# One encoder step on one core: x turned as it lands, its norm folded into the head norms and value copies, gates and late loads behind the first projection units

## The chip, the cores and the metric

The kernel runs on one core of a Trainium2 chip. TensorE does the matrix products and the turns (transposes through a product with the identity), VectorE (DVE), ScalarE (ACT) and GpSimd (POOL) do the rest, and SyncE (SP) issues nearly all DMA transfers. The metric is the device time of one execution in microseconds (us). In the profile PEld is TensorE's weight load, and SPq the issuing of transfers on SyncE.

## The reference

All is float32. 16 meta tokens, 256 prompt rows and 8 x 16 sample rows, 1024 wide, go through one layer:

```
hn = x * rsqrt(mean(x*x) + 1e-6) * attn_norm
fq, fk, fv, ff, dq, dk, dv = split(hn @ w_in)       # 512 512 512 8 512 512 512
fq, fk: rms norm of each of 8 heads of 64, gain;  logf = log_sigmoid(ff + b_forget)
dq, dk: rms norm of each head of 64, gain, rotary;  v as it is
fox:   softmax(q k / 8 + c_q - c_k, causal) v,  c = cumsum(logf)
diff:  (softmax(q1 k1 / 8) - lam softmax(q2 k2 / 8)) v, rms norm;  lam from exp of two dot products
h = x + concat(fox, diff) @ w_out
y = h + top-4-of-32 expert layer (1024 -> 2048 -> 1024) of rms(h)
```

The sample rows also see 256 cached keys and values per batch. Keys, values and logf of all rows are outputs.

## The kernel before

SBUF is one tensor, `arena`, cut by hand. The work stands in program order on each engine, joined by semaphores. There are four row tiles (`TILES`): meta (t = 0, 16 rows), two prompt tiles (t = 1, 2) and the sample tile (t = 3), 128 rows each.

**Opening.** SyncE loads x, the constants (`consts_all`, 0.6 MB, the identity in it), three gain vectors, the eight gate columns of `w_in`, block 0 of `w_in`, small gains, lambda vectors and the rotation, then blocks 1 to 5 (2 MB each, L403), the cached forget gates (L419, 32-byte runs) and the first cache rows (L425). ACT squares and sums each x tile (L687) and takes roots (L690). DVE takes reciprocals and scales x in place (L932). TensorE turns x in blocks of 128 x 128 into PSUM (L1332). ACT and DVE evacuate four blocks each per tile into `hnT`, times the gain column `gcol` (L698, L938). Then TensorE forms the gate products `w_ff` x `hnT` (L1339, 8 rows by 400 columns, 8 chunks), and DVE and ACT make the log sigmoid and its running sum from them.

**Projection.** A list `units` gives the order: blocks 0 to 4 (fox k, fox v, diff k, fox q, diff q), each for t = 1, 2, 3, so units 0 to 2 are fox k, 3 to 5 fox v, 6 to 8 diff k; then the meta tile for four blocks at once (L1375), and block 5 (diff v). A wide unit is 8 chunks of 128 x 128 weights by 512 columns (L1391). A float32 product is two instructions in the profile. For q and k units ACT squares z (L741), DVE sums by head, adds the epsilon (`ss8`, L995), ACT takes the root (L743), DVE inverts, scales z (L998) and multiplies by the gain (L1011); POOL rotates in the diff group (L575 to L579). The result stands in one of two staging buffers `zo`, from which SyncE stores it (L446) and TensorE turns it (`turn_z`, L1351, one unit late). Before writing a `zo`, `free_zo` waits for the turn and the landing of the store that used it last:

```python
if is_n(units[i]):
    eng.wait_ge(z_T, upto(is_n, i + 1))
...
if stores_on(u, o % 2):
    eng.wait_ge(s_store[o % 2], 16 * stores_on(u, o % 2))
```

ACT evacuates the turned k (L718), and for v units it copies z out (L752). `banks[4]` and `banks[5]` take the wide units in turn, so a unit waits until the unit two before it has been read.

**Later stages.** Attention (32 steps, prompt and sample), output projection, routing, and 16 pairs of experts, whose weights (24 MB a pair) run through a ring of eight 2 MB pieces. SyncE's loop refills a piece when TensorE has done with it. None of this is touched.

## Time and profile before

| | us |
|---|---|
| three runs, median (lowest to highest) | 1300.49 (1298.23 to 1304.32) |
| the profiled execution | 1307.11 |
| its span | 1305.2 |
| TensorE busy | 1234.1 (95%) |
| TensorE weight load busy | 548.7 (42%) |
| DVE / ACT / POOL busy | 356.5 / 199.0 / 157.4 |
| HBM read / written | 441.66 MB / 4.86 MB |

Durations come from the profiled execution, one run that was longer than the three timed ones. A matmul's own duration contains its way through the pipeline; a row of several instructions gives the stretch that they took together. "Idle before" is the engine's wait and what ended it.

### The profile page before, as it was taken

Reading aid. Unit: us, or ns where it says so; the run is one execution under the profiler, and the core shown is the slowest. Engines: PE = TensorE matmul, PEld = TensorE weight load, DVE = VectorE, ACT = ScalarE, POOL = GpSimd, SP = SyncE. Lnnn points to the kernel's source line nnn. Section 1 sums busy time; section 2 is a strip of 40 time slices with the busy share of each in tenths; the row PEclk is TensorE's granted clock in tenths of the full one; section 3 lists DMA queues with packets and bytes.
Section 4 is the critical chain, followed back from the end, with each engine's and each line's share of the span. In section 5 each row is a group of like instructions: output and inputs, shape, how many; then the busy total and the mean of one; then the engine's idle time right before and its main releaser. Section 6 shows DMA issues by size and latency. Waiting matters only on the chain.

```text
span 1305.2 us, 16112 instructions
## 1 busy us (share of the span) xinstructions
PE 1234.1 (95%) x6065; PEld 548.7 (42%) x6066; DVE 356.5 (27%) x944; ACT 199.0 (15%) x522; POOL 157.4 (12%) x377
## 2 busy tenths in 40 slices
PE   6799988999899999999999999999999999999997
PEld 3344445654554344343434434343434434343432
DVE  3213446451413122121412212121412212121402
ACT  5111155341401011010101001010100001010100
POOL 0011311110032020210202020120202020120000
PEclk9999997799889999999999999999999999999998
DMA  7900250585349999999999999999999999999993
GB/s 281 344 31 17 94 197 34 192 287 200 119 184 431 427 427 428 428 428 429 428 429 428 428 429 428 427 429 429 426 430 428 427 430 428 428 430 427 426 429 156
DMA packets 54537, 447.06 MB, mean 343 GB/s; under 512 B 10817, under 2 KB 11090, under 8 KB 29922
## 3 DMA queue, kind: packets, MB, share of 16 engines
q1 hardware_dynamic: 54498, 446.54, 82.4%
q8 instruction: 24, 0.39, 0.1%
q14 instruction: 15, 0.12, 0.0%
HBM read 441.66 MB, written 4.86 MB: 342 GB/s over the span
## 4 chain that ended last, share of the span: by engine, by line
PE 64%; DMA 26%; SPq 4%; DVE 2%; issue 1%; ACT 1%; POOL 1%; DVEq 0%; ACTq 0%; POOLq 0%
DMA arena<-in_w_gate_up 24%; PE psum L1685 17%; PE psum L1653 17%; PE psum L1634 7%; PE psum L1391 6%; PE psum L1556 3%; PE psum L1700 2%; SPq L403 2%; PE psum L1668 1%; PE psum L1427 1%; PE psum L1664 1%; DMA arena<-in_cache_diff_k 1%; SPq L419 1%; PE psum L1457 1%; DMA out_fox_k_p<-arena 1%
## 5 line engine op out<-in xcount | busy, mean ns | idle before, releaser
L1653 PE MATMUL psum<-arena 128*64 128x512 f32 x2048 | 450.5, 599 | 20.9 <-DMA arena<-in_w_gate_up 20.3
L1653 PEld LDWEIGHTS psum<-arena 128*64 128x64 f32 x2048 | 153.0, 138 | 316.5 <-issue 316.5
L1685 PE MATMUL psum<-arena 128*64 128x512 f32 x1024 | 224.5, 596 | 0.8
L1288 DVE TENSOR_SCALAR arena<-psum 128x256 f32<-128x256 f32 x64 | 26.7, 418 | 434.1 <-PE psum L1653 432.3
L1685 PEld LDWEIGHTS psum<-arena 128*64 128x64 f32 x1024 | 78.7, 137 | 135.7 <-issue 134.4
L1391 PE MATMUL psum<-arena 128*128 128x512 f32 x288 | 127.6, 599 | 0.0
L890 ACT ACTIVATE arena<-arena 128x256 f32<-128x256 f32 x64 | 26.7, 417 | 632.7 <-DVE arena L1288 632.7
L1634 PEld LDWEIGHTS psum<-arena 128*128 128x128 f32 x768 | 89.8, 197 | 16.1 <-issue 16.1
L1634 PE MATMUL psum<-arena 128*128 128x128 f32 x768 | 92.8, 282 | 3.8 <-POOL arena L642 3.8
L635 POOL COPY arena<-arena 128x6 f32 (+1 forms) x16 | 3.0, 188 | 761.2 <-PE psum L1685 704.6
L1700 PE MATMUL psum<-arena 128*128 128x512 f32 x192 | 93.2, 623 | 0.0
L1391 PEld LDWEIGHTS psum<-arena 128*128 128x128 f32 x288 | 54.3, 193 | 65.3 <-issue 64.6
L1306 DVE TENSOR_TENSOR arena<-psum,arena 128x512 f32<-128x512 f32 x96 | 66.5, 692 | 25.3 <-PE psum L1700 25.3
L1301 DVE COPY arena<-psum 128x512 f32<-128x512 f32 x16 | 11.1, 692 | 219.5 <-PE psum L1685 219.5
L1700 PEld LDWEIGHTS psum<-arena 128*128 128x128 f32 x192 | 28.6, 188 | 64.4 <-DVE arena L1306 42.1
L652 POOL TENSOR_SCALAR arena<-arena 128x64 f32<-128x64 f32 x96 | 53.8, 579 | 0.0
L1556 PE MATMUL psum<-arena 128*128 128x512 f32 x96 | 42.4, 595 | 1.0 <-DVE arena L1155 1.0
L642 POOL TENSOR_SCALAR arena<-arena 128x64 f32<-128x64 f32 x96 | 40.2, 443 | 0.0
L1276 DVE TENSOR_TENSOR arena<-arena 128x256 f32<-128x256 f32 x64 | 36.4, 609 | 5.4
L898 ACT ACTIVATE arena<-psum 128x512 f32<-128x512 f32 x16 | 9.6, 598 | 161.9 <-PE psum L1685 161.9
L994 DVE TENSOR_REDUCE arena<-arena 128x8 f32<-128x512 f32 (+1 forms) x14 | 9.6, 684 | 79.1 <-ACT arena L741 79.1
L1290 DVE SCALAR_TENSOR_TENSOR arena<-arena 128x256 f32<-128x256 f32 x64 | 27.3, 426 | 2.2
(225 smaller groups left out, 827.5 us busy)
## 6 DMA issues: line engine op xcount, KB each, us to landing
arena<-in_w_gate_up SPq DMA_DIRECT2D x128, 2048.0 KB, 25.2
arena<-in_w_down SPq DMA_DIRECT2D x64, 2048.0 KB, 23.0
arena<-in_w_in SPq DMA_DIRECT2D x6, 2048.0 KB, 19.8
arena<-in_cache_fox_k SPq DMA_DIRECT2D x8, 512.0 KB, 7.0
arena<-in_cache_diff_k SPq DMA_DIRECT2D x8, 512.0 KB, 6.8
arena<-in_cache_fox_v SPq DMA_DIRECT2D x8, 512.0 KB, 7.3
arena<-in_cache_diff_v SPq DMA_DIRECT2D x8, 512.0 KB, 9.4
arena<-in_w_out SPq DMA_DIRECT2D x4, 1024.0 KB, 6.2
```

Of the source, the lines that this page charges most:

```text
L642: last = nc.gpsimd.tensor_scalar(sel[u][:, t, cols], C["iota"], pRK[u][:, t, x:x + 1], None, ALU.is_equal)
L652: last = nc.gpsimd.tensor_scalar(selg[u][:, t, cols], C["iota"], pRK[u][:, t, x:x + 1], pG[u][:, t, x:x + 1], ALU.is_equal, ALU.mult)
L890: nc.scalar.activation(sg[n % 2], tg[n % 2], ACT.Sigmoid, scale=1.702).then_inc(sig_ready, 1)
L1276: nc.vector.tensor_tensor(act_rows[:, 32 * n:32 * (n + 1)], ta[n % 2].rearrange("s (p q) -> s p q", q=8), sg[n % 2].rearrange("s (p q) -> ...
L1290: lk(nc.vector.scalar_tensor_tensor(out=ta[n % 2], in0=tl[n % 2], scalar=1.0, in1=tg[n % 2], op0=ALU.add, op1=ALU.mult))
L1306: nc.vector.tensor_tensor(y[:, t, cols], banks[4 + n % 2], y[:, t, cols], ALU.add).then_inc(y_added, 1)
L1391: last = mm(z_bank(u), hnT[:, k, r0:r0 + n], wv[:, k], start=(k == 0), stop=(k == 7))
L1556: last = mm(banks[4 + n % 2], oT[:, k, P * t:P * (t + 1)], wv[:, k % 2, 512 * hf:512 * hf + 512], start=(k == 0), stop=(k == 7))
L1634: last = mm(banks[6 + k // 4][:, P * (k % 4):P * (k % 4 + 1)], x2n[:, t, P * k:P * (k + 1)], sel[u][:, t], start=(t == 0), stop=(t == 2))
L1653: last = mm(banks[n][half], XT[u][:, k, half], piece_slot(s[x])[:, c0:c0 + 512], start=False, stop=(k == 7), skip_group_check=True)
L1685: last = mm(banks[hf][half], actT[:, 4 * i + c, half], w, start=False, stop=(i == 1 and c == 3), skip_group_check=True)
L1700: mm(banks[4 + n % 2], gT[:, P * t:P * (t + 1)], rows[:, 512 * hf:512 * hf + 512], start=True, stop=True).then_inc(scat_done, 1)
```

## The change

- SyncE loads the identity alone first, then x tiles 1 and 2, block 0 in two halves with x tile 3 between, the meta rows eight times (into all 128 partitions), block 1, the other constants, gate columns, forget bias, lambda vectors, rotation, and block 2. Blocks 3, 4, 5 are issued behind the stores of units 0, 1, 2; the cached forget gates at unit 7; cache batch 0 at unit 8, batch 1 at unit 10. The three gain vectors and the four head gains are issued by ACT.
- x is turned unscaled as it lands, in the order 1, 2, 3, 0, tile 3 behind unit 0 and tile 0 behind unit 1. The row norm is not applied to x. The head norm of q and k cancels a row's scale, so only its epsilon is multiplied by (mean(x*x) + eps), as `xeps`; v is multiplied by the inverse root in its copy.
- The gate products come behind unit 2, as four column groups of 32 rows whose halves of the sum are joined and turned by four products with `pick` behind unit 3 (`gate_rows`). The gates then stand with the rows on partitions. ACT's Exp and Ln are behind unit 4, and the running sum is made on TensorE behind unit 6 (`gate_cumulate`) where DVE's scan made it before.

```diff
+X_ORDER = (1, 2, 3, 0)
+LOG_UNIT = 4
...
+    c["pick"] = np.tile(np.eye(E)[:, 0:8], (4, 1))
...
-            sp.dma_start(xs[0][0:META], io["meta_tokens"][:, :]).then_inc(s_x[0], 16)
+            sp.dma_start(ident, io["consts"][:, 0:P]).then_inc(s_ident, 16)
             for t in range(2):
                 sp.dma_start(xs[1 + t], io["x_prompt"][0, P * t:P * (t + 1), :]).then_inc(s_x[1 + t], 16)
-            sp.dma_start(xs[3], io["x_sample"].rearrange("b i n -> (b i) n")).then_inc(s_x[3], 16)
-            sp.dma_start(consts_all, io["consts"][:, :]).then_inc(s_const, 16)
-            for i, (name, n) in enumerate((("attn_norm", 8), ("ffn_norm", 8), ("diff_out_norm", 1))):
-                sp.dma_start(vecs[8 * i:8 * i + n], io[name][0].rearrange("(k p) -> k p", p=P)).then_inc(s_vec, 16)
-            sp.dma_start(gcol_x, io["ffn_norm"][0].rearrange("(p k) -> p k", p=P)).then_inc(s_gx, 16)
-
             def load_w_in(bi):
                 c0 = BLOCKS[bi][0]
                 sp.dma_start(slot(2 * bi, 2).rearrange("p (k n) -> p k n", k=8),
                              io["w_in"][0, :, c0:c0 + W].rearrange("(k p) n -> p k n", p=P)).then_inc(s_win[bi], 16)
 
+            def load_first(k0, arrived):
+                c0 = BLOCKS[0][0]
+                sp.dma_start(slot(k0 // 4).rearrange("p (k n) -> p k n", k=4),
+                             io["w_in"][0, P * k0:P * (k0 + 4), c0:c0 + W].rearrange("(k p) n -> p k n", p=P)
+                             ).then_inc(arrived, 16)
+
+            load_first(0, s_win[0])
+            sp.dma_start(xs[3], io["x_sample"].rearrange("b i n -> (b i) n")).then_inc(s_x[3], 16)
+            load_first(4, s_win0b)
+            for j in range(8):
+                sp.dma_start(xs[0][META * j:META * (j + 1)], io["meta_tokens"][:, :]).then_inc(s_x[0], 16)
+            load_w_in(1)
+            sp.dma_start(consts_all[:, P:], io["consts"][:, P:]).then_inc(s_const, 16)
             with nc.allow_non_contiguous_dma(reason="eight columns of w_in"):
-                sp.dma_start(nb_ff[0:8, 0:1], io["b_forget"][0].rearrange("(h o) -> h o", o=1)).then_inc(s_wff, 16)
-                sp.dma_start(w_ff, io["w_in"][0, :, 1536:1544].rearrange("(k p) n -> p k n", p=P)).then_inc(s_wff, 16)
-            load_w_in(0)
-            for i, name in enumerate(("fox_q_norm", "fox_k_norm", "diff_q_norm", "diff_k_norm")):
-                sp.dma_start(gains[:, i], io[name][0].partition_broadcast(P)).then_inc(s_small, 16)
+                sp.wait_ge(wff_zero, 1)
+                sp.dma_start(w_ff[:, :, 0:8], io["w_in"][0, :, 1536:1544].rearrange("(k p) n -> p k n", p=P)
+                             ).then_inc(s_wff, 16)
+            sp.dma_start(b_ff, io["b_forget"][0].partition_broadcast(P)).then_inc(s_bff, 16)
             for i, name in enumerate(("lambda_q1", "lambda_k1", "lambda_q2", "lambda_k2")):
                 sp.dma_start(lamv[:, i], io[name][0].partition_broadcast(P)).then_inc(s_small, 16)
             sp.dma_start(rot.rearrange("p t c h -> p (t c h)"), io["rot"][:, :]).then_inc(s_rot, 16)
+            load_w_in(2)
...
+            sp.dma_start(gcol_x, io["ffn_norm"][0].rearrange("(p k) -> p k", p=P)).then_inc(s_gx, 16)
...
-            for bi in range(1, 6):
-                load_w_in(bi)
-            for t in range(2):
-                sp.dma_start(lf_cache[:, t], io["cache_fox_logf"][0, :, P * t:P * (t + 1)].rearrange("b p h -> p b h")
-                             ).then_inc(s_lfc, 16)
...
-            load_cache(0, "k")
-            load_cache(0, "v")
...
+                if u < 3:
+                    load_w_in(3 + u)
+                if u == 7:
+                    for t_ in range(2):
+                        sp.dma_start(lf_cache[:, t_], io["cache_fox_logf"][0, :, P * t_:P * (t_ + 1)].rearrange("b p h -> p b h")
+                                     ).then_inc(s_lfc, 16)
+                if u == 8:
+                    load_cache(0, "k")
+                    load_cache(0, "v")
+                if u == 10:
                     sp.wait_ge(xT_done, 4)
+                    sp.wait_ge(sq_done, 2)
                     load_cache(1, "k")
                     load_cache(1, "v")
                 if u == 6:
-                    sp.wait_ge(lf_ready, 2)
+                    sp.wait_ge(lf_ready, 1)
...
+            nc.gpsimd.memset(w_ff.rearrange("p k n -> p (k n)"), 0.0).then_inc(wff_zero, 1)
...
+            for i, (name, n) in enumerate((("attn_norm", 8), ("ffn_norm", 8), ("diff_out_norm", 1))):
+                ac.dma_start(vecs[8 * i:8 * i + n], io[name][0].rearrange("(k p) -> k p", p=P)).then_inc(s_vec, 16)
+            for i, name in enumerate(("fox_q_norm", "fox_k_norm", "diff_q_norm", "diff_k_norm")):
+                ac.dma_start(gains[:, i], io[name][0].partition_broadcast(P)).then_inc(s_gains, 16)
...
-            for t in range(4):
-                n = TILES[t][1]
-                ac.wait_ge(s_x[t], 16)
-                link(nc.scalar.activation(junk[0:n], xs[t][0:n], ACT.Square, accum_out=stat[0:n, t:t + 1]))
-            nc.scalar.activation(stat[:, 8:9], stat[:, 8:9], ACT.Square).then_inc(sq_done, 1)
-            ac.wait_ge(ms_done, 1)
-            nc.scalar.activation(stat[:, 4:8], stat[:, 0:4], ACT.Sqrt).then_inc(rt_done, 1)
...
+            def x_squares(t):
+                ac.wait_ge(s_x[t], 16 if t else 128)
+                return nc.scalar.activation(junk if t else xs[0], xs[t], ACT.Square, accum_out=stat[:, t:t + 1])
+
+            for t in (1, 2):
+                hn_evac(t)
+            for t in (1, 2, 3):
+                link(x_squares(t))
+            nc.scalar.activation(stat[:, 8:9], stat[:, 8:9], ACT.Square).then_inc(sq_done, 1)
+            ac.wait_ge(ms_done, 1)
+            nc.scalar.activation(stat[:, 5:8], stat[:, 1:4], ACT.Sqrt).then_inc(rt_done, 1)
+            hn_evac(3)
+
+            def meta_rows():
+
+                hn_evac(0)
+                link(x_squares(0))
+                nc.scalar.activation(stat[:, 45:46], stat[:, 45:46], ACT.Square).then_inc(sq_done, 1)
+                ac.wait_ge(ms_done, 2)
+                nc.scalar.activation(stat[:, 4:5], stat[:, 0:1], ACT.Sqrt).then_inc(rt_done, 1)
+
+            def log_gates():
+
+                for f, i in ((ACT.Exp, 1), (ACT.Ln, 2)):
+                    ac.wait_ge(lg_v, i)
+                    nc.scalar.activation(ffl, ffl, f).then_inc(lg_a, 1)
+                    if i == 1:
+                        ac.wait_ge(lam_v, 1)
+                        nc.scalar.activation(stat[:, 10:12], stat[:, 10:12], ACT.Exp).then_inc(lam_a, 1)
...
-                    nc.scalar.activation(dst, z, ACT.Copy).then_inc(z_copied, 1)
+                    nc.scalar.activation(dst, z, ACT.Copy, scale=stat[rw, t:t + 1]).then_inc(z_copied, 1)
...
+                if u == 1:
+                    meta_rows()
+                if u == LOG_UNIT:
+                    log_gates()
...
-            for t in range(4):
-                n = TILES[t][1]
-                nc.vector.tensor_scalar(xs[t][0:n], xs[t][0:n], stat[0:n, t:t + 1], None, ALU.mult).then_inc(xn_done, 1)
...
+            def x_scales(n_, c):
+
+                cols = slice(c[0], c[-1] + 1)
+                ve.wait_ge(sq_done, n_)
+                nc.vector.tensor_scalar(stat[:, cols], stat[:, cols], 1.0 / D, EPS, ALU.mult, ALU.add).then_inc(ms_done, 1)
+                ve.wait_ge(ms_done, n_)
+                link(nc.vector.tensor_scalar(xeps[:, cols], stat[:, cols], EPS, None, ALU.mult))
+                ve.wait_ge(rt_done, n_)
+                link(nc.vector.reciprocal(stat[:, cols], stat[:, 4 + c[0]:5 + c[-1]]))
+                nc.vector.tensor_copy(stat[:, 9:10], stat[:, 8:9]).then_inc(x_scale, 1)
+
+            for t in (1, 2):
+                hn_evac(t)
+            x_scales(1, (1, 2, 3))
+            hn_evac(3)
...
+            def gate_logits():
+
+                ve.wait_ge(ff_done, 1)
+                link(nc.vector.memset(ffv, 0.0))
+                nc.vector.tensor_copy(ffc, banks[6][:, 0:NTOK]).then_inc(ff_copied, 1)
+                ve.wait_ge(ffn_done, 1)
+                ve.wait_ge(s_bff, 16)
+                for t_ in range(4):
+                    n_ = TILES[t_][1]
+                    ins = nc.vector.scalar_tensor_tensor(out=ffv[0:n_, t_], in0=banks[6][0:n_, 448 + 8 * t_:456 + 8 * t_],
+                                                         scalar=stat[0:n_, t_:t_ + 1], in1=b_ff[0:n_],
+                                                         op0=ALU.mult, op1=ALU.add)
+                link(ins)
+                link(nc.vector.tensor_scalar(ffl, ffv, -1.0, None, ALU.mult))
+                nc.vector.tensor_tensor(ffl, ffl, ffv, ALU.min).then_inc(lg_v, 1)
+
+            def gate_logs():
+
+                ve.wait_ge(lg_a, 1)
+                nc.vector.tensor_scalar(ffl, ffl, 1.0, None, ALU.add).then_inc(lg_v, 1)
+                ve.wait_ge(lg_a, 2)
+                link(nc.vector.tensor_scalar(ffv, ffv, 0.0, None, ALU.min))
+                nc.vector.tensor_tensor(lf, ffv, ffl, ALU.subtract).then_inc(lf_ready, 1)
+                ve.wait_ge(lf_ready, 1)
+                nc.vector.tensor_copy(lf_new[0:META], lf[0:META, 0:1].to_broadcast([META, 8, 8])).then_inc(lf_ready, 1)
+
+            def gate_sums():
+
+                ve.wait_ge(ncp_done, 1)
+                link(nc.vector.tensor_copy(nc_p[0:8], banks[6][0:8, 0:NKEY_P]))
+                nc.vector.tensor_copy(nc_p[32:40], nc_p[0:8]).then_inc(lf_ready, 1)
...
-                nc.vector.tensor_scalar(ss8[rw, 0], ss8[rw, 0], 1.0 / HD, EPS, ALU.mult, ALU.add).then_inc(z_ms, 1)
+                nc.vector.tensor_scalar(ss8[rw, 0], ss8[rw, 0], 1.0 / HD, xeps[rw, t:t + 1], ALU.mult, ALU.add
+                                        ).then_inc(z_ms, 1)
...
+                    hn_evac(0)
+                    x_scales(2, (0,))
+                if m == 2:
+                    lambdas()
+                    gate_logits()
+                    gate_logs()
+                    lambda_maps()
+                if m == 3:
+                    gate_sums()
...
-            pe.wait_ge(gcol_done, 1)
-            for t in range(4):
+
+            def turn_x(t):
                 n = TILES[t][1]
-                pe.wait_ge(xn_done, t + 1)
+                pe.wait_ge(s_x[t], 16 if t else 128)
                 for k in range(8):
                     last = nc.tensor.transpose(banks[2 * t + k // 4][:, P * (k % 4):P * (k % 4) + n],
                                                xs[t][0:n, P * k:P * (k + 1)], ident[0:n, 0:n])
                 last.then_inc(xT_done, 1)
-            pe.wait_ge(hnT_a, 4)
-            pe.wait_ge(hnT_v, 4)
-            pe.wait_ge(s_wff, 32)
-            for k in range(8):
-                last = mm(banks[6][0:8, 0:NTOK], w_ff[:, k], hnT[:, k], start=(k == 0), stop=(k == 7))
-            last.then_inc(ff_done, 1)
+
+            for t in (1, 2):
+                turn_x(t)
+
+            def gate_products():
+
+                pe.wait_ge(hnT_a, 4)
+                pe.wait_ge(hnT_v, 4)
+                pe.wait_ge(s_wff, 16)
+                for k in range(8):
+                    j = k % 4
+                    last = mm(banks[6][32 * j:32 * j + 32, 0:NTOK], w_ff[:, k], hnT[:, k], start=(k < 4), stop=(k >= 4))
+                last.then_inc(ff_done, 1)
+
+            def gate_rows():
+
+                pe.wait_ge(ff_copied, 1)
+                pe.wait_ge(s_const, 16)
+                for t_ in range(4):
+                    r0, n = TILES[t_]
+                    last = mm(banks[6][0:n, 448 + 8 * t_:456 + 8 * t_], ffc[:, r0:r0 + n], C["pick"], start=True, stop=True)
+                last.then_inc(ffn_done, 1)
+
+            def gate_cumulate():
+
+                pe.wait_ge(lf_ready, 1)
+                R, later = banks[6][0:8], C["cumul"][:, P:P + 1]
+                mm(R[:, 0:META], lf[0:META, 0], C["cumul"][0:META, 0:META], start=True, stop=False, skip_group_check=True)
+                mm(R[:, META:NKEY_P], lf[0:META, 0], later[0:META].to_broadcast([META, SEQ]), start=True, stop=False,
+                   skip_group_check=True)
+                mm(R[:, META:META + P], lf[:, 1], C["cumul"][:, 0:P], start=False, stop=False, skip_group_check=True)
+                mm(R[:, META + P:NKEY_P], lf[:, 1], later.to_broadcast([P, P]), start=False, stop=False,
+                   skip_group_check=True)
+                mm(R[:, META + P:NKEY_P], lf[:, 2], C["cumul"][:, 0:P], start=False, stop=True,
+                   skip_group_check=True).then_inc(ncp_done, 1)
...
+                    if u < 3:
+                        pe.wait_ge(hnT_a, u + 1)
+                        pe.wait_ge(hnT_v, u + 1)
+                    if u in (0, 1):
+                        pe.wait_ge(hnT_a, 2)
+                        pe.wait_ge(hnT_v, 2)
...
+                        if u == 0 and k == 4:
+                            pe.wait_ge(s_win0b, 16)
...
+                if u in (0, 1):
+                    turn_x((3, 0)[u])
+                if u == 2:
+                    gate_products()
+                if u == 3:
+                    gate_rows()
+                if u == 6:
+                    gate_cumulate()
```

## Rows read from the trace of the kernel before

**Rows 1.** Windows: busy us (x instructions) of each engine, granted clock, DMA share, GB/s.
```profile
6.00:8.00 2.00, 0.00 (x0) 0.00 (x0) 0.00 (x0) 1.81 (x5) 0.00 (x0) 1.00 0.99 385
...
54.00:63.30 9.30, 1.07 (x6) 1.04 (x6) 0.85 (x2) 1.09 (x2) 0.00 (x0) 0.78 1.03 355
...
64.00:66.00 2.00, 2.00 (x4) 0.94 (x3) 0.00 (x0) 0.00 (x0) 0.00 (x0) 0.50 0.86 329
66.00:68.00 2.00, 2.00 (x5) 0.83 (x5) 0.00 (x0) 0.00 (x0) 0.00 (x0) 0.97 0.07 27
...
178.40:212.00 33.60, 26.80 (x219) 16.57 (x219) 21.84 (x107) 22.52 (x83) 2.47 (x9) 1.00 0.19 63
212.00:242.00 30.00, 28.94 (x120) 18.71 (x123) 14.29 (x51) 11.12 (x46) 6.39 (x22) 0.51 0.21 72
...
370.00:1305.20 935.20, 905.34 (x4348) 371.26 (x4344) 214.25 (x455) 76.91 (x178) 97.41 (x243) 0.99 0.98 415
```
**Rows 2.** The chain that ended last: start us, us, what.
```profile
41.08 6.35 SPq L419
...
52.14 9.26 DMA out_fox_k_p<-arena
...
63.38 22.04 PE psum L1391 x48
...
132.09 6.87 PE psum L1391 x16
...
822.60 28.93 DMA arena<-in_w_gate_up
```
**Rows 3.** Timeline of all engines: start us, us, engine, line, operation, [idle before <-releaser].
```profile
2.92 1.28 ACT L687 ACT_TABLE_LOAD   x1 [2.79 <-DMA arena<-in_meta_tokens]
...
7.88 1.06 ACT L687 ACTIVATE arena<-arena 128x1024 f32<-128x1024 f32 x1 [0.15 <-DMA arena<-in_x_sample]
...
11.03 2.73 DVE L932 TENSOR_SCALAR arena<-arena 16x1024 f32<-16x1024 f32 x4
...
61.52 0.69 DVE L1011 TENSOR_TENSOR arena<-arena 128x512 f32<-128x512 f32 x1 [12.02 <-DMA out_fox_k_p<-arena]
...
62.27 1.11 PE L1351 MATMUL psum<-arena 128*128 128x128 f32 x4 [8.23 <-DVE arena L1011]
```
**Rows 4.** Timeline of TensorE's matmuls alone.
```profile
9.95 0.26 PE L1326 MATMUL psum<-arena 17*128 17x17 f32 x1 [9.95 <-DMA arena<-in_diff_out_norm]
11.92 6.32 PE L1332 MATMUL psum<-arena 16*128 16x16 f32 x32 [1.71 <-DVE arena L932]
19.50 5.55 PE L1339 MATMUL psum<-arena 128*8 128x400 f32 x16 [1.27 <-ACT arena L698]
24.98 14.00 PE L1391 MATMUL psum<-arena 128*128 128x512 f32 x32
38.91 0.36 PE L1399 MATMUL psum<-arena 8*16 8x8 f32 x4
...
148.25 7.06 PE L1375 MATMUL psum<-arena 128*16 128x512 f32 x64
```
**Rows 5.** Groups by form (busy us, mean ns), and one line's instructions (min/median/max ns).
```profile
L1332 PE MATMUL psum<-arena 128*128 128x128 f32 x24 | 5.4, 423 | 0.0
...
L698 ACT ACTIVATE arena<-psum,arena 128x128 f32<-128x128 f32 x12 | 3.4, 369 | 2.2 <-PE psum L1332 2.2
...
L1351 PE MATMUL psum<-arena x56: 207/273/475, 39.2 to 178.2; 128*128 128x128 f32 x48, 16*128 16x16 f32 x8
```
**Rows 6.** SyncE's queue (start us, us to issue), and the landing of in_x_prompt.
```profile
1.22 0.88 SPq L394 DMA_DIRECT2D arena<-in_x_prompt  x2
...
3.98 0.25 SPq L398 DMA_DIRECT2D arena<-in_diff_out_norm  x1
...
6.55 2.64 SPq L411 DMA_DIRECT2D arena<-in_fox_q_norm  x1
...
DMA to landing us min/median/max: 3.3/3.7/4.2
```

More of the change, by code:

```diff
@@ L40 @@
 Y_BASE = 6
-CONSTS = [("ident", 128), ("eye4", 32), ("smask", 16), ("ones", 128), ("iota", 64), ("own", 128), ("maps", 2),
+X_ORDER = (1, 2, 3, 0)
+LOG_UNIT = 4
+CONSTS = [("ident", 128), ("eye4", 32), ("pick", 8), ("smask", 16), ("ones", 128), ("iota", 64), ("own", 128), ("maps", 2),
           ("cumul", 130), ("cumul_s", 288), ("offs", 8), ("causal", 128), ("chunk", 128)]
@@ L130, in build @@
         lf = at3(take(32), 4, 8)
-        w_ff = at3(take(64), 8, 8)
-        nb_ff = at(take(2), 2)
+        take(66)
         ncs = at(lf0, NKEY_S)
@@ L943, in _ @@
+            for t in (1, 2):
+                hn_evac(t)
+            x_scales(1, (1, 2, 3))
+            hn_evac(3)
+            ve.wait_ge(s_gains, 16 * 4)
             for i in (0, 2):
                 link(nc.vector.tensor_scalar(gains[:, i], gains[:, i], HD ** -0.5, None, ALU.mult))
[L947 to L950 removed]
@@ L969, in _, with lambdas @@
-            link(nc.vector.tensor_scalar(stat[:, 11:12], stat[:, 11:12], -LAM_INIT, None, ALU.add))
-            link(nc.vector.tensor_scalar(gcol[:, 16:17], gcol[:, 16:17], 1.0 - LAM_INIT, None, ALU.mult))
-            link(nc.vector.scalar_tensor_tensor(out=C["maps"][:, 0:1], in0=C["maps"][:, 1:2], scalar=stat[:, 11:12],
-                                                in1=C["maps"][:, 0:1], op0=ALU.mult, op1=ALU.add))
-            nc.vector.tensor_scalar(comb, comb, C["maps"][:, 0:1], None, ALU.mult).then_inc(comb_ready, 1)
+            def lambdas():
+                ve.wait_ge(s_small, 16 * 5)
+                for i in range(2):
+                    link(nc.vector.tensor_tensor(lamv[:, 2 * i], lamv[:, 2 * i], lamv[:, 2 * i + 1], ALU.mult))
+                    link(nc.vector.tensor_reduce(stat[:, 10 + i:11 + i], lamv[:, 2 * i], AX.X, ALU.add))
+                nc.vector.tensor_copy(stat[:, 9:10], stat[:, 8:9]).then_inc(lam_v, 1)
@@ L1394, in _ @@
                     late.append(u)
-                if u == 1:
-                    pe.wait_ge(lf_ready, 1)
-                    for t_ in range(4):
-                        a, b = TILES[t_]
-                        last = nc.tensor.transpose(banks[6][0:b, 448 + 8 * t_:456 + 8 * t_], ffl[0:8, a:a + b], ident[0:8, 0:8])
-                    last.then_inc(lfT_done, 1)
                 if u in TABLE_AT:
```

71 lines of the change are left out of this document (25 added, 46 removed).

## The prediction

> **What bounds the kernel now.** I read the windows first, cut where the program changes stage [rows 1]. Expert stage, 370 us to the end: the DMA engines are busy 0.98 of the time at 415 GB/s and TensorE 905 of 935 us; the chain of waits passes through weight transfers of nearly 29 us in each expert pair [rows 2]. Both limits of that stage are untouched. It starts when attention is over, so what is saved before it should move it forward one for one. Next the front. The reader is to see three things. From 24.98 us the wide projection units run back to back on TensorE at 7.0 us each (32 matmul instructions in 14.00) [rows 4]. Before that TensorE does little: the vector turn at 9.95, the x turns from 11.92, the gate products from 19.50 to 25.05 [rows 4]. And between 54.0 and 62.3 us it stands still for 8.23 us [rows 1, 3]. For that gap follow the chain back: the turn of unit 2 waits for DVE's gain product, which waited 12.02 us for its staging buffer, which waits for the landing of unit 0's key store; SyncE issued this store only at 52.14, behind the weight loads and the cached forget gates (the second L419 issue alone holds the queue 6.35 us), and its landing took 9.26 us on the chain [rows 2, 3]. So up to 63.38, where unit 4 begins, the length is set by the opening chain plus this stall, and after it by TensorE's own work.
>
> The clock needs care. The granted column says 1.00 from the start, even at 6 to 8 us where TensorE has not yet run [rows 1], but the x turns there last 423 ns each (mean of the 24 full ones), while the same form of turn in L1351 has a median of 273 ns and a maximum of 475 ns, the latter in the half-clock stretch after the gap [rows 5]. I read the opening turns as run at 1.2 GHz, with no record before the first change; the gate products from 19.50 run at 2.4 GHz (16 instructions of 400 columns in 5.55 us, 0.347 us each) [rows 4]. After the 8.23 us gap the clock is 0.50 until just after 66 us [rows 1].
>
> **The change, part by part: when unit 0 starts.** Gone from before the x turns: the squares of all x tiles, the root, and four scalings (2.73 us on DVE, starting at 11.03) [rows 3]. The turn of tile 1 now needs only the identity (first on the queue), x and the vectors. x tile 1 lands 3.3 us after its issue at 1.22, tile 2 at 1.68 + 4.2 = 5.9 us [rows 6]. The vectors move to ACT's queue, issued by about 2.1 us (SyncE takes some 0.4 us an issue); I take them at 5.0. Bounds: a first small transfer on an empty queue, the meta tokens, landed 2.1 us after its issue at 0.77 (at 2.9 [rows 3]), and the last vector, issued at 3.98 behind bulk, arrived at 9.9 [rows 4, 6], 5.9 us later; so 4.2 to 8.0. Vector turn 0.26, then eight turns, 1.7 us (6.32 us for 32 [rows 4], of which the eight of the meta tile are shorter): tile 1 done at 7.0, tile 2 at 8.7. ACT loads its table after its wait (1.28 us [rows 3]), so the gains column is there at about 6.8; the evacuations are 3.4 / 12 x 4 = 1.1 us per tile [rows 5], done at 8.2 and 9.9. **Unit 0 starts at 10.0 instead of 24.98.** If the vectors come at 8.0 it is 12.9; if ACT's seven issues meet a queue that holds an issue for 2.64 us as L411 was held [rows 6], it is 11.6.
>
> Weights: the first half of block 0 is the fourth transfer. After x tile 2 (5.9) it needs 1.05 MB at 385 GB/s [rows 1], 2.7 us: 8.6, then x tile 3 at 10.0, the second half at 12.7, 13.5 with the small transfers of ACT's queue between. Tile 3 landed at 7.88 before [rows 3], so those numbers are of the right size.
>
> **Unit 0 to unit 4.** Unit 0 begins cold: in the stretch after the gap the clock came back 3.7 to 3.9 us after work resumed (62.27 to just after 66) [rows 1, 3]. Half speed for 3.5 us does two of eight chunks, the other six take 5.3: end at 18.8. If it were warm: 3.5 us, a wait for the second half until 13.7, 3.5 more, 17.2. Then the turns of x tile 3 (eight at full clock, half of twice the 1.11 us that four took at the low one [rows 3]: 1.1), unit 1 (7.0), the turns of z 0 and of the meta tile (1.4): 28.3; unit 2: 35.3; turn 0.5. The gate products now write four groups of 32 rows. The trace has that pattern: the meta unit's 64 instructions of 512 columns, four column groups, took 7.06 us, the time of 16 full ones [rows 4]. So I price them at 5.55 / 4 = 1.4 us, not 5.55 (the other bound). 37.2; unit 3: 44.2; turn 0.5; the new gate rows: eight instructions with full 128-column weights, 1.6 us (bounds 0.36, the four small turns they replace [rows 4], and eight at L1351's 273 ns = 2.2 [rows 5]; their weights are as wide as those of L1351, so I go towards the upper). **Unit 4 starts at 46.3 instead of 63.38: 17.1 us.** ACT and DVE finish the first normalisations, scales and meta rows beside units 1 and 2; unit 2 needs z 0 read, a chain of some 5 us inside the 7 us of unit 1.
>
> The DVE gate chain (copy, scale and bias, log) and ACT's two logs with their table loads lie beside units 4 and 5, which are value units that DVE does not touch; the cumulative sum needs them only after unit 6. ACT must load Exp, Ln and the root table again, 3 x 1.28 us, inside 14 us: cover holds; without it, up to 4 us.
>
> **After unit 4.** The half-clock piece goes: 22.04 us for three units [rows 2] against 3 x 6.88 = 20.6 (the length of a unit later in that view), minus 1.4. The cumulation on TensorE is new: ten instructions, 656 columns twice, at 0.87 ns a column from the gate products = 1.1, with short ones 1.3 (bounds 0.6 and 3.4). The scan on DVE that it replaces was hidden. The value copies with a scale operand and the epsilon as an operand: nothing, same shapes.
>
> **Queues.** The store of unit 0 now stands behind block 2, the lambdas and the rotation. Bytes up to block 2: 9.0 MB, landed at about 3.5 + 9.0/0.385 = 27 us; the store is needed free at unit 2's gain product, about 39. Block 3 goes behind it and is needed at unit 9. At u = 7 and 8 the forget gates (twice about 6 us of queue) and 2 MB of cache stand between key stores of the differential group; each store's buffer is next wanted two units later by the rotation, over 14 us. No stall expected; if one of them takes the place of the old, its price is that of the old, 8 to 9 us.
>
> Sum: 17.1 + 1.4 - 1.3 = 17.2 us saved. The profiled execution took 1307.11 us (span 1305.2, 1.9 around it), so 1289.9 in its terms; that execution is 6.6 above the median of 1300.49, to which I apply the same difference: **1283 us**.
>
> **A rule weighed.** The row on opening turns says 423 ns a turn, through 6.32 us of continuous turns [rows 4, 5]. The Trainium skill, "TensorE: Matmul & The Clock Gate", PE-mode transpose, says that transposes do not count as activity for the clock. By that rule unit 0 starts at the low clock, as I took it (18.8); by the granted column alone it would be 17.2, and the sum 1.6 us better.
>
> **Rivals.** (a) *The stall moves*: a store or the second half of block 0 is late, or DVE waits in the gate code; 8 to 9 us come back: 1292. For it: the queue is full for long (355 GB/s through the stall [rows 1]), and new waits stand on DVE with four units queued behind them. Against: the arithmetic above leaves 10 us of slack. 0.13. (b) *The clock in attention*: 178 to 212 us shows TensorE 26.8 of 33.6 us busy, then 30 us at 0.51 [rows 1]. Shifted by 17 us, the fall may come elsewhere: full clock there would give up to 10 (TensorE's 29 busy us would be 14.5, but ACT and DVE take over): 1273, 0.07. A second such stretch, or unit 0 to 3 largely at half clock: 1295, 0.05. (c) *The other side: ACT's queue issues block its compute.* ACT issues seven transfers before its first evacuation. L411 was held 2.64 us with one block queued, and later issues behind full blocks 5 to 6 us (L419) [rows 2, 6]. If the seven are each held 5 us, unit 0 starts at 0.8 + 35 + 3 = 39 us, later than before; the point where all gain is lost is 10 + 17.2 = 27 us, where slower begins (by 0.5%, 34). I have ACT's issues out before block 1 is queued, so 0.03: 1307. A place beside it: the Trainium skill, "DMA: Bandwidth & Descriptors", Issuing engines are not separate DMA queues, says that both queues run on the same engines and only issue time is saved; no row here has two queues at work.
> (d) *My sum*: 0.72, own range 1277 to 1289.
>
> **Numbers.** 1283. The range from (b) low and (a) high with the spread of the runs shown: 1275 to 1293. Under 0.5% (6.5 us, what a measurement of this kernel tells from no change): faster 0.89, same 0.08 (parts of a and b), slower 0.03.
>
> **What would show it.** Unit 0's matmuls at 10 us; unit 4 at 46; no idle time over 2 us on TensorE up to the end of the projections, which end near 161 instead of 178 us; gate products in about 1.4 us; the granted clock full through the projections; the expert stage of unchanged length, 17 us earlier. Wrong if DVE's L1011 counterpart or the turn after it shows a DMA as releaser again, if TensorE waits more than 3 us for either half of block 0, or if the attention stage changes length.

## The result, and the profile after

| | before | changed | predicted |
|---|---|---|---|
| median, us | 1300.24 (4 runs, 1298.23 to 1304.32) | 1286.15 (4 runs, 1281.32 to 1290.47) | 1283 (1275 to 1293) |
| profiled execution, us | 1307.11 | 1290.47 | 1289.9 |
| its span, us | 1305.2 | 1288.7 | |

The ratio of the changed kernel to the one before is 0.9867, with a 95% interval of 0.9825 to 0.991: 14.1 us by the medians, 16.6 us between the two profiled executions, where 17.2 was forecast. In microseconds of the median of before the interval is 11.7 to 22.8, so the time agrees with the sum but can't test its terms. The traces can: the projections ended 15.7 us earlier, not 17.2, because the start of unit 0, unit 0 itself and the value copies were priced too low, and attention, for which the sum had nothing, became 1.4 us shorter. That the total came so close is partly luck.

In TensorE's timeline of before, unit 4 is the first unit of this piece (the chain of [rows 2] counts the same unit from 63.38):

```profile
63.17 29.10 PE L1391 MATMUL psum<-arena 128*128 128x512 f32 x64
```

TensorE's matmuls in the changed kernel, to be read against [rows 4] (start us, us, what, idle before and its releaser):

```profile
4.72 0.26 PE L1404 MATMUL psum<-arena 17*128 17x17 f32 x1 [4.72 <-DMA arena<-in_diff_out_norm]
4.91 3.57 PE L1410 MATMUL psum<-arena 128*128 128x128 f32 x16
12.23 5.10 PE L1506 MATMUL psum<-arena 128*128 128x512 f32 x8 [3.75 <-DMA arena<-in_w_in]
18.04 3.70 PE L1506 MATMUL psum<-arena 128*128 128x512 f32 x8 [0.71 <-DMA arena<-in_w_in]
21.58 1.04 PE L1410 MATMUL psum<-arena 128*128 128x128 f32 x8
...
37.94 1.55 PE L1424 MATMUL psum<-arena 128*32 128x400 f32 x16
...
46.93 0.97 PE L1433 MATMUL psum<-arena 128*16 128x8 f32 x8
47.75 20.85 PE L1506 MATMUL psum<-arena 128*128 128x512 f32 x48
...
155.23 7.13 PE L1506 MATMUL psum<-arena 128*128 128x512 f32 x16 [0.55 <-ACT arena L792]
```

The 8.23 us gap of [rows 3] is gone: from the start of the piece at 18.04 to 146 us TensorE has no wait over 0.5 us. Unit 4 starts at 47.75 instead of 63.17, 15.4 us earlier. But unit 0 does not start at 10.0, as the sum had it, it starts at 12.23 after 3.75 us without work, its first half takes 5.10 us, and the second half of block 0 comes only at 18.0. The last line is a new wait: the projection unit that waits for ACT's scaled value copies.

Windows of the changed kernel, for [rows 1] (busy us (x instructions) of PE, PEld, DVE, ACT, POOL, then granted clock, DMA share, GB/s):

```profile
6.00:8.00 2.00, 2.00 (x12) 2.00 (x11) 1.00 (x4) 1.56 (x6) 0.00 (x0) 1.00 0.60 204
...
12.00:14.00 2.00, 1.77 (x2) 0.84 (x3) 0.00 (x0) 0.35 (x1) 0.00 (x0) 0.50 1.06 408
...
18.00:20.00 2.00, 1.96 (x5) 1.01 (x6) 0.00 (x0) 0.00 (x0) 0.00 (x0) 1.00 1.04 230
...
196.00:226.00 30.00, 29.10 (x173) 18.49 (x174) 17.22 (x60) 12.44 (x52) 7.41 (x25) 0.72 0.20 71
...
355.00:1288.70 933.70, 903.86 (x4340) 370.73 (x4336) 212.40 (x447) 77.02 (x178) 95.86 (x240) 0.99 0.98 415
```

From 6 to 8 us the DMA engines are busy only 0.60 and move 204 GB/s, where they moved 385 before [rows 1]. From 12 to 14 us the granted clock is 0.50. The attention stage still has its half-clock stretch, now from 196 us, and the expert stage is as before, only earlier. In the chain its first matmuls stand at 343.53 us instead of 360.58, 17.0 us earlier, and the span ends 16.5 earlier: of what was saved in front 0.5 us was lost behind.

### The profile page after: what moved, and what is told of

It is laid out like the page before. It is cut to its first block, busy times and chain, and to the rows that moved or that the text cites. A ratio compares the mean times of both kernels' runs of the same rounds, so it can differ in the third digit from the quotient of the medians.

```text
span 1288.7 us, 16163 instructions
## 1 busy us (share of the span) xinstructions
PE 1229.9 (95%) x6079; PEld 545.4 (42%) x6080; DVE 354.7 (28%) x947; ACT 198.4 (15%) x523; POOL 158.3 (12%) x378
## 4 chain that ended last, share of the span: by engine, by line
PE 67%; DMA 27%; DVE 3%; ACT 1%; issue 1%; POOL 1%; SPq 1%; ACTq 0%; POOLq 0%; DVEq 0%
DMA arena<-in_w_gate_up 24%; PE psum L1801 17%; PE psum L1769 17%; PE psum L1506 8%; PE psum L1750 7%; PE psum L1672 3%; PE psum L1816 2%; PE psum L1784 1%; PE psum L1780 1%; DMA arena<-in_w_in 1%; PE psum L1543 1%; DMA arena<-in_cache_diff_k 1%; PE psum L1640 1%; PE psum L1573 1%; PE psum L1561 1%
## 5 line engine op out<-in xcount | busy, mean ns | idle before, releaser
L1750 PEld LDWEIGHTS psum<-arena 128*128 128x128 f32 x768 | 89.8, 197 | 16.1 <-issue 16.1
L1506 PEld LDWEIGHTS psum<-arena 128*128 128x128 f32 x288 | 53.9, 192 | 70.3 <-issue 63.3
L1816 PEld LDWEIGHTS psum<-arena 128*128 128x128 f32 x192 | 28.6, 188 | 64.3 <-DVE arena L1384 42.1
L1672 PEld LDWEIGHTS psum<-arena 128*128 128x128 f32 x96 | 17.8, 190 | 22.1 <-issue 20.6
```

What stands on the lines that cost most here:

```text
L1506: last = mm(z_bank(u), hnT[:, k, r0:r0 + n], wv[:, k], start=(k == 0), stop=(k == 7))
L1672: last = mm(banks[4 + n % 2], oT[:, k, P * t:P * (t + 1)], wv[:, k % 2, 512 * hf:512 * hf + 512], start=(k == 0), stop=(k == 7))
L1750: last = mm(banks[6 + k // 4][:, P * (k % 4):P * (k % 4 + 1)], x2n[:, t, P * k:P * (k + 1)], sel[u][:, t], start=(t == 0), stop=(t == 2))
L1816: mm(banks[4 + n % 2], gT[:, P * t:P * (t + 1)], rows[:, 512 * hf:512 * hf + 512], start=True, stop=True).then_inc(scat_done, 1)
```

## The experiments

### The two halves of the change apart

The first kernel is the one before with only the late loads; the second is the changed one with only those undone. Comment lines in the cuts stand for code left out here.

```diff
 # c1_before_late_loads: SyncE, kernel before
-            for bi in range(1, 6):
+            for bi in range(1, 3):
                 load_w_in(bi)
-            # forget gates, load_cache(0, "k"), load_cache(0, "v")
...
+                if u < 3:
+                    load_w_in(3 + u)
+                # u == 7: forget gates; u == 8: cache batch 0; u == 10: batch 1
```

> The kernel before with one part of the change alone: blocks 3 to 5 behind the first key stores, forget gates and cache rows at units 7, 8 and 10. Theory (the stall of 8.2 us is the store's place in the queue, the opening is separate): the gap at 54 us is gone, the clock stays up, the span falls by 8.2 + 1.4, some 9.5 us; the opening up to 24.98 is the same. Rival (the opening and the stall are one chain): the gain is under 4 us, because units 3 to 5 then wait for their weights.

It took 0.9918 of before (0.9884 to 0.9952), 10 runs against 23, medians 1292.06 and 1302.09. Its TensorE timeline:

```profile
24.37 14.00 PE L1394 MATMUL psum<-arena 128*128 128x512 f32 x32
...
46.39 7.03 PE L1394 MATMUL psum<-arena 128*128 128x512 f32 x16
53.26 0.60 PE L1354 MATMUL psum<-arena 128*128 128x128 f32 x4
53.69 21.62 PE L1394 MATMUL psum<-arena 128*128 128x512 f32 x50
```

Unit 4 follows unit 3 at once, at 53.69 instead of 63.17: 9.5 us, of which 0.6 comes from a slightly earlier opening in that run, so 8.9. The stall was the store's place in the queue, and taking it away is worth 10.0 us of the median by itself. The rival, under 4 us, falls.

```diff
 # u1_loads_ahead: SyncE, changed kernel
             load_w_in(2)
+            for bi in range(3, 6):
+                load_w_in(bi)
+            # forget gates here; load_cache(0, "k"), load_cache(0, "v") ahead of the unit loop
...
-                if u < 3:
-                    load_w_in(3 + u)
```

> The changed kernel with that part undone: blocks 3 to 5, forget gates and cache batch 0 issued before the first store again, the new opening kept. Theory: unit 2's gain product waits for the landing of unit 0's store again, which now comes some 55 to 60 us, while TensorE gets there 7 us earlier than before; 12 to 15 us slower than the changed kernel, so near the time of the kernel before (within 0.3% of it), and the whole new opening is then worth almost nothing. Rival (parts add up): 9 us slower, still 7 us faster than before.

1.0041 of before (1.0007 to 1.0074): the whole new opening is worth nothing with the store behind the loads. It is even a little worse than the time of before, and further from the changed kernel than the 12 to 15 us expected: by the two ratios some 23 us. TensorE's timeline in this variant:

```profile
39.33 7.13 PE L1505 MATMUL psum<-arena 128*128 128x512 f32 x16
63.93 1.12 PE L1457 MATMUL psum<-arena 128*128 128x128 f32 x4 [17.46 <-DVE arena L1086]
65.86 1.60 PE L1432 MATMUL psum<-arena 128*16 128x8 f32 x8 [0.81 <-DVE arena L1021]
```

The chain that led to the wait, same run (start us, us, what):

```profile
49.41 3.36 SPq L437
...
55.31 7.74 DMA out_fox_k_p<-arena
```

In the chain SPq is SyncE's issue of L437. Unit 3 ends 7.6 us earlier than before, but the store issues at 55.31, when the queue lets it (52.14 before [rows 2]), so the wait grows from 8.2 to 17.5 us. Unit 4 starts at 67.3, 4.1 us later than before and 19.6 later than in the changed kernel. The rival, that the parts add up, falls: the opening pays only if the stall is gone.

### Why block 0 is late

The sum had put its halves at 8.6 and 13.5 us; they came at 12.2 and 18.0. Two parts of the change load the engines there: the gains on ACT's queue, and the eight meta transfers.

Meta late alone, on SyncE's queue:

```diff
+            load_w_in(1)
             for j in range(8):
                 sp.dma_start(xs[0][META * j:META * (j + 1)], io["meta_tokens"][:, :]).then_inc(s_x[0], 16)
-            load_w_in(1)
```

> The changed kernel with the eight meta transfers moved behind block 1. In its trace block 0's second half lands at 18.0 us, where 13.5 was expected; from 14 to 20 us the engines are over 1.0 busy at 227 to 244 GB/s. Theory A (the meta pieces, 16 partitions each, run at half rate and share the engines with what is still under way): the second half lands at 14 to 15 us, unit 0 ends 3 us earlier. Theory B (something else in the opening holds the rate down, the small gain transfers on ACT's queue): still 17 to 18 us.

Unit 0 in TensorE's timeline of that variant, then a window around it, same run:

```profile
12.05 10.15 PE L1506 MATMUL psum<-arena 128*128 128x512 f32 x16 [3.74 <-DMA arena<-in_w_in]
```

```profile
12.00:18.00 6.00, 5.95 (x7) 2.52 (x8) 0.67 (x4) 2.84 (x5) 0.00 (x0) 0.50 1.05 393
```

Both theories were half right. The first half is still at 12.05. The second is no longer waited for, and the engines move 393 GB/s from 12 to 18 us (293 in the changed kernel over the same stretch), so the meta pieces did hold it up. But unit 0 ends at 22.04, no earlier than the 21.6 of the changed kernel, because it now runs whole at the low clock. One execution, 1287.04 us.

Gains late alone, from ACT's queue to SyncE's behind block 1:

```diff
             load_w_in(1)
+            for i, name in enumerate(("fox_q_norm", "fox_k_norm", "diff_q_norm", "diff_k_norm")):
+                sp.dma_start(gains[:, i], io[name][0].partition_broadcast(P)).then_inc(s_gains, 16)
...
-            for i, name in enumerate(("fox_q_norm", "fox_k_norm", "diff_q_norm", "diff_k_norm")):
-                ac.dma_start(gains[:, i], io[name][0].partition_broadcast(P)).then_inc(s_gains, 16)
```

> The changed kernel with only the four head gains moved from ACT's queue to SyncE's behind block 1; the meta transfers stay where they are. Theory B, now the one in front: the four gain transfers (128 rows of 256 bytes each) beside the bulk hold the rate at 200 GB/s between 6 and 8 us; without them block 0's first half lands by 9.9 us, TensorE does not fall to the low clock, and unit 0 takes 7.1 us. The meta transfers were queued behind block 0's second half and should not delay it: unit 4 at 43.5 to 44.5 us. Rival (both moves are needed): unit 0 has a wait of 2 us or more for the second half, unit 4 at 46.

TensorE's timeline with the gains late:

```profile
9.99 3.67 PE L1506 MATMUL psum<-arena 128*128 128x512 f32 x8 [1.44 <-ACT arena L716]
14.35 3.70 PE L1506 MATMUL psum<-arena 128*128 128x512 f32 x8 [0.69 <-DMA arena<-in_w_in]
```

This is it: unit 0 starts at 9.99, released by ACT's evacuation and no more by a transfer, at the full clock. The second half is still waited for, 0.69 us. From 6 to 8 us 351 GB/s are moved. Unit 4 starts at 44.27, 3.5 us earlier than in the changed kernel; the one execution took 1283.79 us (span 1281.9). The edit changes three things at once, the queue of the gains, their moment, and what runs beside their 256-byte rows. That the gains at that place hold block 0 up is shown; which of the three does it is not.

Both late:

> Meta transfers and the four head gains both behind block 1 (the gains on SyncE's queue again). Theory B: the first half lands at 9 to 10 us instead of 12.2, the second at 12 to 13, TensorE does not fall to the low clock before unit 0, and unit 4 starts at 43 to 44 instead of 47.75; 3 to 4 us faster than the changed kernel. If only A holds: first half still at 12 us, 3 us faster at most.

TensorE's timeline with both late, then one window of the same run:

```profile
9.88 7.10 PE L1506 MATMUL psum<-arena 128*128 128x512 f32 x16 [1.44 <-ACT arena L716]
...
43.48 20.85 PE L1506 MATMUL psum<-arena 128*128 128x512 f32 x48
```

```profile
6.00:8.00 2.00, 2.00 (x11) 2.00 (x10) 1.13 (x4) 1.53 (x6) 0.00 (x0) 1.00 1.05 407
```

407 GB/s from 6 to 8 us against 204 in the changed kernel; unit 0 in one piece; unit 4 at 43.48, 4.3 us earlier than in the changed kernel. 0.9841 of before (0.9796 to 0.9885), median 1280.82; timed again,

> Meta transfers and head gains behind block 1, timed again so that it stands beside the two filled variants on one chip: 0.984 of before.

it was 0.9866 (0.9828 to 0.9903), median 1283.39. The changed kernel itself, again:

> The changed kernel itself, timed again beside the kernel before. If the spread of single runs (1281 to 1290) is the clock in the attention stage, the same spread shows here, runs with a higher mean granted clock are the shorter ones, and the ratio to before is 0.987 as in the first comparison.

0.9873 (0.9827 to 0.9918), median 1287.49, single runs from 1281.21 to 1292.84. Of its six runs the two with the highest granted clock (0.979 and 0.980) are the shortest and the one with the lowest (0.968) the longest, as expected. The intervals of the two kernels overlap, so the timing can't tell them apart, and the traces differ among themselves: unit 4 is at 47.75 and 46.63 in two traces of the changed kernel, at 43.48 and 45.40 in two of both late.

### The clock in front of unit 0

Four products of the identity with 512 columns of x, into unused `banks[7]`, on top of meta late:

```diff
             for t in (1, 2):
                 turn_x(t)
+            for _ in range(4):
+                mm(banks[7][:, 0:512], ident, xs[1][:, 0:512], start=True, stop=True)
```

> The variant with the meta transfers late (block 0 arrives at 12.0 us, unit 0 then took 10.15 us at the low clock) with four extra 512-column products of the identity and x tile 1 into an unused PSUM bank, between the turns of x tile 2 and unit 0. Theory (idle time of 3.7 us lets the clock fall, and the low clock costs unit 0 3 us): the clock stays at 1.00, unit 0 starts at 12.1 and takes 7.1 to 7.5 us, unit 4 starts at 45.2 instead of 48.2. Rival (the clock is low anyway, the turns don't raise it): the extra products take 1.7 us each, and unit 0 starts after 15 us.

TensorE's timeline of this variant, then a window, same run:

```profile
9.37 3.90 PE L1417 MATMUL psum<-arena 128*128 128x512 f32 x8
13.10 7.03 PE L1508 MATMUL psum<-arena 128*128 128x512 f32 x16
```

```profile
12.00:18.00 6.00, 6.00 (x15) 2.65 (x15) 0.67 (x4) 3.81 (x7) 0.00 (x0) 1.00 1.05 393
```

The clock stays at 1.00 and unit 0 takes 7.03 us instead of 10.15. The eight instructions of the extra products took 3.90 us, one of them 0.89 us and at least half of them 0.59, so the clock was up at the latest just after the turns. It started 1.0 us later than hoped, since x tile 1 landed later in that run (turns from 5.90 instead of 4.89), and unit 4 is at 46.15, 2.1 us before the variant without them. The low clock cost unit 0 3.1 us.

A short wait does not make unit 0 warm by itself. Here it is in the second timing of both late, then a window, same run:

```profile
10.22 9.17 PE L1506 MATMUL psum<-arena 128*128 128x512 f32 x16 [1.44 <-ACT arena L716]
```

```profile
10.00:12.00 2.00, 1.78 (x2) 0.84 (x3) 0.00 (x0) 1.97 (x4) 0.00 (x0) 1.00 1.05 399
```

The kernel and the wait of 1.44 us are those of the first trace, but unit 0 takes 9.17 us instead of 7.10, and unit 4 starts at 45.40 instead of 43.48. Single instructions take up to 1192 ns, where the full clock gives 592. The granted column says 1.00 all the same, as it does for the opening turns that the prediction read as run at 1.2 GHz, so for this piece the durations decide. Six traces have block 0 in time. In three (gains late, both late, the first full fill below) unit 0 ran at the full clock; in the other three (both late again, the full fill again, the even steps) it began at the low one and took 9.17, 8.58 and 9.24 us. In all six TensorE did the same work before it; what decides between them was not tried.

### The scale operand of the value copies

```diff
-                    nc.scalar.activation(dst, z, ACT.Copy, scale=stat[rw, t:t + 1]).then_inc(z_copied, 1)
+                    nc.scalar.activation(dst, z, ACT.Copy).then_inc(z_copied, 1)
```

> The changed kernel with the value copies on ACT without their scale operand; this leaves the row norm out of the values. The scaled 512-column copy takes 0.69 us in the changed kernel's trace, the plain one took 0.59 to 0.60 in the trace of before. Theory (the scale operand costs 0.1 us a copy and puts ACT in front of the last projection unit and of attention): the copies take 0.59, TensorE's wait of 0.55 us before the last unit is gone, and from the meta unit's start to the first score product it is 0.6 to 0.9 us shorter (31.1 us in the changed kernel). Rival: the length of the copy comes from elsewhere and stays 0.69.

L792 in the changed kernel (ns min/median/max, then from when to when in us):

```profile
L792 ACT ACTIVATE arena<-psum,arena x8: 681/688/692, 46.6 to 163.4; 128x512 f32<-128x512 f32 x6, 16x512 f32<-16x512 f32 x2
```

The same line without the scale operand:

```profile
L792 ACT ACTIVATE arena<-psum x8: 589/598/605, 47.2 to 163.3; 128x512 f32<-128x512 f32 x6, 16x512 f32<-16x512 f32 x2
```

And TensorE's timeline there, the last two units:

```profile
148.11 14.18 PE L1506 MATMUL psum<-arena 128*128 128x512 f32 x32
```

0.09 us a copy, and the two units run as one piece. From the meta unit's start to the first score product it is 30.5 us (132.46 to 162.95) against 31.1 (131.90 to 163.03), 0.6 us, at the lower edge of what was expected. The routing of the expert layer depends on the values, so nothing behind attention compares; its total time (1539.92) is not used.

### The clock in attention

The single runs of before reach from 1294.43 us at a mean granted clock of 0.979 to 1312.47 at 0.963 (23 runs beside the first experiments). A line through span against the time at the low clock, taken as 2 x (1 - clock) x span, has 0.33 us a microsecond. That is a correlation. To try it, TensorE got work in its waits in prompt attention, on top of both late:

```diff
+                if x["where"] == "p" and i >= 3:
+                    pe.wait_ge(mix_copied, copy_no[i - 3])
+                    for _ in range(3):
+                        mm(banks[6 + (i - 1) % 2][:, 384:512], ident, ident, start=True, stop=True, skip_group_check=True)
                 pe.wait_ge(normed, i + 1)
```

> Both groups of transfers late, and in 13 of the 16 prompt steps of attention three more 128-column products (0.66 us in all) into a free part of a PSUM bank, in TensorE's wait for the evacuated turns (0.9 us every second step). Theory (TensorE's low load from 160 to 195 us lets the clock fall for the 16 to 30 us that follow): the clock stays at 1.00 through the prompt steps, 4 to 8 us faster than the variant without the fill, so 0.979 of before or less, and single runs spread less. Rival (the fall has nothing to do with idle slots, or the fill costs more than it holds): the low stretch is still there and the time is 0 to 6 us longer.

0.9825 (0.9784 to 0.9866), median 1281.67, not the 0.979 expected, and beside 0.9841 for both late on another chip no gain clear of the noise. Again, and in even steps only:

> The same with three extra products in 13 prompt steps. In its first trace the low clock from 185 to 215 us was gone, but a pair of steps took 5.6 us where it takes 5.1 at the full clock without them. Theory (the fill gives back some 4 us of what it saves): 2 us faster than without the fill, not separable. Rival (it holds the clock for good): 5 us or more faster.

> The extra products only in the even steps from step 4 on (six times 0.66 us), where TensorE's wait of 0.9 us is. Theory: a pair of steps stays at 5.1 to 5.2 us and the clock stays at 1.00 through the prompt steps: 4 to 7 us faster than without the fill, 0.980 of before. Rival (half the fill doesn't hold the clock): the low stretch is back, time as without the fill.

Two windows without the fill (the second timing of both late):

```profile
160.00:184.00 24.00, 19.20 (x164) 11.92 (x164) 14.25 (x71) 16.49 (x55) 0.89 (x5) 1.00 0.25 87
184.00:216.00 32.00, 28.18 (x163) 17.46 (x162) 19.71 (x84) 15.74 (x67) 6.85 (x22) 0.79 0.11 36
```

With the full fill (its second timing):

```profile
160.00:184.00 24.00, 21.33 (x180) 14.26 (x181) 13.99 (x69) 16.18 (x54) 0.87 (x5) 1.00 0.22 74
184.00:216.00 32.00, 30.92 (x234) 22.46 (x232) 21.72 (x89) 17.44 (x73) 7.11 (x24) 1.00 0.18 65
```

With the even steps alone:

```profile
184.00:216.00 32.00, 30.27 (x166) 20.23 (x164) 18.49 (x80) 15.20 (x66) 5.93 (x19) 0.73 0.09 34
```

At the full clock, from 160 to 184 us, TensorE is busy 19.20 of 24 us without the fill and 21.33 with it. The busy share of the later window can't be set beside that without care: where the clock is low, the same work counts as more busy time. With all 13 steps filled the clock stays at 1.00 from 184 to 216 us, in both traces; with six it does not, against what was expected, though TensorE had more to do there than without the fill. The fill costs 0.5 us a pair of steps (5.6 instead of 5.1 us from one score product to the next but one). Times on one chip: 0.9866 without, 0.9826 (0.9793 to 0.9859) with the full fill, 0.9843 (0.9809 to 0.9876) with the even steps; medians 1283.39, 1278.60, 1282.66. The full fill has the lowest median and a mean granted clock of 0.984 to 0.989 in every run of both its timings, both late without it 0.965 to 0.983. That it holds the clock is shown; that it is faster is likely, but the intervals overlap. It is the best version found, 1278.60 against the changed kernel's 1287.49 timed on another chip.

## Why the prediction held, step by step

- **The stall goes, 8 to 9 us, and nothing takes its place.** Right, and shown alone: 8.9 us in the trace, 0.9918 in time. The gate chain and the queue behind units 7 and 8 brought no wait, as argued.
- **Unit 0 starts at 10.0.** Wrong: 12.23. The vectors were there at 4.7 and ACT was not held (the 2.64 us row had no counterpart before 3.4 us), so both bounds that I had drawn were the wrong ones. What failed is the term for block 0, 1.05 MB at 385 GB/s: it took the rate of the bulk alone, 385 GB/s, for a stretch that it shares with four small broadcasts, where the trace has 204. With the gains moved away unit 0 starts at 9.99.
- **Second half at 13.5.** Wrong: 18.0, first by the same 3.6 us, then by the meta transfers, which I had taken to be behind it and harmless.
- **Unit 0 begins cold.** Right in effect, not in cause. In the changed kernel's trace the clock was up before unit 0 (0.92 from 10 to 12 us, 0.50 from 12 to 14) and fell in the wait of 3.75 us that my sum did not have. With the block there in time unit 0 ran warm in three traces (7.10 us in one piece) and began cold in three (8.58 to 9.24 us, where I had 8.8). Where it ran warm, nearly all of TensorE's work before it was turns. So my reading of the Trainium skill, "TensorE: Matmul & The Clock Gate", PE-mode transpose, gave the right number here, but its rule that transposes don't count for the clock does not hold in those three traces; the other three are as it would have them.
- **Gate products 1.4, gate rows 1.6, cumulation 1.3.** Measured 1.55, 0.97 and 1.33. The column groups run side by side, as the meta unit's row said. The rows ran shorter than the row that I went by, by 0.8 us to the start of unit 4.
- **The value copies cost nothing.** Wrong by 0.09 us each, which put ACT in front of the last unit: 0.6 us.
- **Sum.** Unit 4 started at 47.75, not 46.3: unit 0 began 2.2 us late and took 0.6 more, the rest took 1.3 less. In one and the same view that is 15.4 us earlier than before (63.17); my 17.1 was counted from the chain's 63.38. From there to the end of the projections before takes 115.2 us (178.36 - 63.17) and the changed kernel 115.0 (162.71 - 47.75). Inside it the half-clock piece gives 1.3 (22.04 against 20.70 us in the chains) and the waits for GpSimd (1.02 and 0.58 us before, one of 0.46 after) 1.1, which I had not seen, against 1.3 for the cumulation and 0.6 for the value copies. So the projections ended 15.7 us earlier, not 17.2. From the first score product to the first expert matmul the changed kernel takes 180.5 us instead of 181.9, so 1.4 came back. Its low-clock stretch stands at another place there; that this is the reason was not tried. The two errors nearly cancel, which is luck and no merit of the sum.
- **Rivals.** (c) did not happen. Of (a) the late second half of block 0 did, but TensorE's wait for it was 0.71 us and not 8 to 9. (b) is real, in both kernels: the single runs of before spread by 18 us (1294.43 to 1312.47) along their granted clock, more than the gain.
- **The signs.** One sign of being wrong came: TensorE waited 3.75 us for the first half of block 0, where I had drawn the line at 3. And the attention stage did change its length, by the 1.4 us above. The time held; the way to unit 0 did not.

## What to carry to other kernels

Where a load queue runs in order, look first for the small store or load whose landing an engine waits for, and put it before the bulk: here this alone was worth 8.9 us up to unit 4 and the new opening 6.5 more (15.4 in all), and without it the new opening was worth nothing. In an opening that is short of bytes, issue small broadcasts only when the first operands have landed, and check for each wait that a change leaves on TensorE whether the clock falls in it. When single runs differ, look at the granted clock of each before comparing medians.

## What the runs showed of the hardware

- With four transfers of 128 rows of 256 bytes on a second queue the rate from 6 to 8 us was 204 GB/s with the engines only 0.60 busy; with them moved behind block 1 on the first queue it was 351 (gains late) and 407 (both late). They themselves took 5.7 to 9.6 us to land. The Trainium skill, "DMA: Bandwidth & Descriptors", Issuing engines are not separate DMA queues, says that the queues interleave on the same engines and that only issue time is saved; the trace agrees that nothing was won in rate, and shows that rate was lost. Whether it is the second queue or the small rows at that moment was not separated.
- Eight transfers of 16 partitions each (64 KB, rows of 4 KB): while they were in flight the engines were over 1.0 busy at 227 to 244 GB/s; with them moved away, 393. Whether their narrow set of partitions or their small size is the reason was not tried.
- After 3.75 us idle ahead of unit 0 the granted clock was 0.50 from 12 to 14 us; after 1.44 us unit 0 ran at the full clock in three traces (gains late, both late, the first full fill) and began at the low one in three others (8.58 to 9.24 us), where the column shows 1.00 throughout; after 2.60 us (the changed kernel timed again) it was 0.78 from 12 to 14 and 0.50 from 14 to 16 us, and unit 0 took 8.83 us.
- In prompt attention the clock fell in every trace without the full fill; in the one shown TensorE was busy 19.20 of 24 us ahead of the fall. In both traces with the full fill (21.33 of 24 us in the one shown) it stayed at 1.00 from 184 to 216 us.
- An ACT copy of 128 x 512 out of PSUM takes 0.69 us with a scale operand and 0.60 without.
